# One-hots of the gate products: from keys outermost, eight tokens innermost, to token by token with the keys innermost

## The reference, cut to what matters

```python
q = (x @ w_q).reshape(T, PEER_HEADS, 2, PEER_DQ_HALF)
s = jnp.einsum('thpd,hpnd->thpn', q, sub_keys)
s1, i1 = lax.top_k(s[:, :, 0], PEER_TOPK)          # 16 of 128 keys, first half
s2, i2 = lax.top_k(s[:, :, 1], PEER_TOPK)          # 16 of 128 keys, second half
cand = s1[..., :, None] + s2[..., None, :]         # 256 sums per head
best, pos = lax.top_k(cand, PEER_TOPK)             # 16 experts per head, 8 heads
gate = jax.nn.softmax(best, axis=-1)
# per token 128 experts with index i1*128 + i2 and a gate
hb = gelu(einsum('tkd,td->tk', u[ids], xb))
out = einsum('tk,tkd->td', gate * hb, v[ids])
```

## Time and profile before

| | us |
|---|---|
| median of 3 runs | 4818.61 (4805.46 to 4823.8) |
| profiled execution | 4822.23 |
| its span, first to last instruction | 4820.7 |
| TensorE busy | 4335.7 (90%) |
| VectorE busy | 3214.2 (67%) |
| ScalarE busy | 1013.3 (21%) |
| gate stage of layer 0, about | 1438 to 1763 |
| gate stage of layer 1, about | 3666 to 3992 |

### The profile page before, as it was taken

How to read it: one execution, slowest core, us unless ns; L and a number is a source line. 1 busy time by engine, 2 the same in 40 slices (tenths; PEclk the granted TensorE clock), 3 DMA queues, 4 the chain that set the end, 5 groups by cost and what they waited for, 6 DMA issues and landing times. The chain is left out here.

```text
span 4820.7 us, 54964 instructions
## 1 busy us (share of the span) xinstructions
PE 4335.7 (90%) x19374; PEld 2495.3 (52%) x19374; DVE 3214.2 (67%) x6400; ACT 1013.3 (21%) x1581; POOL 712.3 (15%) x548
## 2 busy tenths in 40 slices
PE   8999998978979989999998877987778998989998
PEld 5777674645545545544444555554444554534443
DVE  1666652678978867766563675369997886866664
ACT  2111101122224431100001253213333441100000
POOL 0000000002221112222210000001221112322220
PEclk9999999989989999999999999999999999999999
DMA  4111141149877779999991100116776779999995
GB/s 146 38 40 39 39 134 56 54 164 356 322 296 263 282 285 387 374 377 391 394 363 65 33 1 31 44 52 234 284 281 234 281 276 352 400 392 390 392 402 196
DMA packets 291813, 1101.75 MB, mean 229 GB/s; under 512 B 30704, under 2 KB 131184, under 8 KB 222576
## 3 DMA queue, kind: packets, MB, share of 16 engines
q0 software_dynamic: 74752, 539.00, 28.4%
q1 hardware_dynamic: 148272, 336.40, 19.8%
q10 hardware_dynamic: 68544, 223.12, 12.0%
HBM read 1005.61 MB, written 92.80 MB: 228 GB/s over the span
## 5 line engine op out<-in xcount | busy, mean ns | idle before, releaser
L774 POOL DMA_INDIRECT room_p<-in_uv,ga_eidx_p x512 | 694.6, 1357 | 3308.1 <-DVEq L801 2106.5
L1311 PE MATMUL ex_psF_p<-ex_vst_p,ex_gh_p 128*128 128x512 f32 x1920 | 841.3, 593 | 18.4 <-DVE ex_gh_p L1405 18.4
L800 DVE SCALAR_TENSOR_TENSOR ga_acc_p<-room_p,ga_gw_p,ga_acc_p 128x1024 f32<-128x1024 f32 x504 | 625.2, 1282 | 21.5 <-issue 1.3
L786 DVE CUSTOM_DVE_ANT_0 room_p<-room_p,hx_p 128x1024 f32<-128x1024 f32 x512 | 605.6, 1220 | 8.9 <-DMA room_p<-in_uv,ga_eidx_p 4.9
L1311 PEld LDWEIGHTS ex_psF_p<-ex_vst_p,ex_gh_p 128*128 128x128 f32 x1920 | 363.3, 190 | 458.4 <-issue 454.0
L1311 PE MATMUL ex_psF_p<-ex_ust_p,ex_gh_p 128*128 128x512 f32 x1152 | 504.3, 596 | 14.3 <-DVE ex_gh_p L1405 14.3
L891 PE MATMUL eh_psH_sl_p<-h_hi_p,eh_uhi_sl_p 128*128 128x384 bf16 x1056 | 365.5, 346 | 164.9 <-DVE eh_ulo_sl_p L855 164.7
L1311 PEld LDWEIGHTS ex_psF_p<-ex_ust_p,ex_gh_p 128*128 128x128 f32 x1152 | 219.4, 191 | 294.4 <-issue 294.4
L891 PE MATMUL eh_psH_sl_p<-h_lo_p,eh_uhi_sl_p 128*128 128x384 bf16 x1056 | 364.1, 345 | 0.0
L891 PE MATMUL eh_psH_sl_p<-h_hi_p,eh_ulo_sl_p 128*128 128x384 bf16 x1056 | 363.4, 344 | 0.0
L1179 PE MATMUL gt_ps_p<-gt_ohh_p,gt_oh_p 128*128 128x128 bf16 x768 | 300.0, 391 | 51.5 <-DVEq L1164 51.5
(11 more groups left out here) (248 smaller groups left out, 6374.7 us busy)
## 6 DMA issues: line engine op xcount, KB each, us to landing
ex_vst_p<-in_uv ACTq DMA_DIRECT2D x160, 512.0 KB, 8.3
eh_ust_sl_p<-in_uT SPq DMA_DIRECT2D x132, 512.0 KB, 5.5
gates<-gt_gs_p ACTq DMA_DIRECT2D x24, 2048.0 KB, 7.9
ex_gst_p<-gates SPq DMA_DIRECT2D x128, 384.0 KB, 14.7
ex_ust_p<-in_uv ACTq DMA_DIRECT2D x96, 512.0 KB, 8.5
ex_est_p<-hidden SPq DMA_DIRECT2D x196, 192.0 KB, 14.7
eh_ust_gt_p<-in_uT SPq DMA_DIRECT2D x64, 512.0 KB, 6.6
ex_ust_p<-in_uT SPq DMA_DIRECT2D x60, 512.0 KB, 8.7
```

What stands on the lines that cost most here:

```text
L774: self.nc.gpsimd.indirect_dma_start(self.slot[s % self.RING], None, self.uv, bass.IndirectOffsetOnAxis(self.eidx[:, s:s + 1], 0)).then_inc ...
L786: nc.vector.tensor_tensor_reduce(out=row, in0=row, in1=self.hx[:, s // W, :], scale=1.0, scalar=0.0, op0=ALU.mult, op1=ALU.add, accum_out= ...
L800: nc.vector.scalar_tensor_tensor(acc[:], row, self.gw[:, s:s + 1], acc[:], op0=ALU.mult, op1=ALU.add)
L1311: last = nc.tensor.matmul(psF[:, t, x, :], gh[n % 3][:, P * t:P * t + P], vbuf[vslot[n]][:, BANK * x:BANK * x + BANK], start=(n == 0), sto ...
```

## The change

The keys are kept once, `[P, 128]`, in place of eight copies. The one-hots become `[partition, token, key]`, so the operand of token x, `[:, x, :]`, is 128 neighbouring bf16 elements. On VectorE the two sources of the compare change roles: before, the row of eight token values was repeated for every key (an outer repeat) against the replicated keys; now each token value is repeated 128 times innermost, and the row of keys is repeated for every token. In the two multiplications the gate part is repeated innermost in the same way. Counts of instructions, elements and matmuls, their order, and all waits stay as they are.

```diff
-        keys = sb("gt_keys", [P, NK, TI])
-        oh2 = [sb(f"gt_oh2{r}", [P, NK, TI]) for r in range(3)]
-        oh1 = sb("gt_oh1", [P, NK, TI])
+        keys = sb("gt_keys", [P, NK])
+        oh2 = [sb(f"gt_oh2{r}", [P, TI, NK]) for r in range(3)]
+        oh1 = sb("gt_oh1", [P, TI, NK])
...
-            nc.vector.tensor_copy(keys[:], cst.iota[:].unsqueeze(2).to_broadcast([P, NK, TI]))
+            nc.vector.tensor_copy(keys[:], cst.iota[:])
+            every = keys[:].unsqueeze(1).to_broadcast([P, TI, NK])
...
-                part = [pk[:, j, TI * n:TI * n + TI].unsqueeze(1).to_broadcast([P, NK, TI]) for j in range(4)]
-                nc.vector.tensor_tensor(oh1[:], part[0], keys[:], ALU.is_equal)
+                part = [pk[:, j, TI * n:TI * n + TI].unsqueeze(2).to_broadcast([P, TI, NK]) for j in range(4)]
+                nc.vector.tensor_tensor(oh1[:], part[0], every, ALU.is_equal)
...
-                nc.vector.tensor_tensor(oh2[n % 3][:], part[1], keys[:], ALU.is_equal)
+                nc.vector.tensor_tensor(oh2[n % 3][:], part[1], every, ALU.is_equal)
                 dve.drain()
                 nc.vector.tensor_tensor(ohh[n % 3][:], oh1[:], part[2], ALU.mult)
                 nc.vector.tensor_tensor(ohl[n % 3][:], oh1[:], part[3], ALU.mult)
...
-                    nc.tensor.matmul(o, oh2[n % 3][:, :, x], ohh[n % 3][:, :, x], start=True, stop=False)
+                    nc.tensor.matmul(o, oh2[n % 3][:, x, :], ohh[n % 3][:, x, :], start=True, stop=False)
...
-                    last = nc.tensor.matmul(o, oh2[n % 3][:, :, x], ohl[n % 3][:, :, x], start=False, stop=True)
+                    last = nc.tensor.matmul(o, oh2[n % 3][:, x, :], ohl[n % 3][:, x, :], start=False, stop=True)
```

More of the change, by code:

```diff
@@ L1130, in peer_gates @@
         sem = lambda n: nc.alloc_semaphore(n + tag)
-        keys = sb("gt_keys", [P, NK, TI])
-        oh2 = [sb(f"gt_oh2{r}", [P, NK, TI]) for r in range(3)]
-        oh1 = sb("gt_oh1", [P, NK, TI])
-        ohh = [sb(f"gt_ohh{r}", [P, NK, TI]) for r in range(3)]
-        ohl = [sb(f"gt_ohl{r}", [P, NK, TI]) for r in range(3)]
+        keys = sb("gt_keys", [P, NK])
+        oh2 = [sb(f"gt_oh2{r}", [P, TI, NK]) for r in range(3)]
+        oh1 = sb("gt_oh1", [P, TI, NK])
+        ohh = [sb(f"gt_ohh{r}", [P, TI, NK]) for r in range(3)]
+        ohl = [sb(f"gt_ohl{r}", [P, TI, NK]) for r in range(3)]
         gs = [sb(f"gt_gs{s}", [P, NK, TB], F32) for s in range(2)]
```

## The result

The changed kernel takes 4948.6 us (median, 4946.21 to 4952.81), against 4815.5 for the kernel before (median of four runs, the three of the table before and one more): a ratio of 1.0278, 95% interval 1.0256 to 1.030. Its profiled execution takes 4950.4 us, with a span of 4948.9. So the span grew by 128.2 us, where +115 had been worked out.

A forecast was written before the change was run, and what follows sets the result against it. TensorE was taken to bound the gate stages, VectorE some 60 us behind, then VectorE after the change. Stages of +56.4 and +56.1 us plus 3 us of remaining waits gave +115 on 4818.6: 4934 us, range 4904 to 4970.

The forecast's parts named there:

- The price of the one-hots: VectorE's four one-hot instructions: each goes from 688 to 1226 ns, adding 103.3 us per gate stage.
- the upper of two bounds: One-hot instruction on VectorE: 1226 ns if the pace of two elements is lost, against 688 ns if it survives.
- Who is late: Gate stages: VectorE becomes the limit at 7.75 us per unit, against 4.2 (at most 6.2) for TensorE.
- the 1 to 2 us put for what might stay: Gate stages: VectorE's waits for ScalarE that remain, 1 to 2 us per stage.
- TensorE's gain: Gate matmuls with contiguous operands: some 100 us less per stage, all but the last unit's share turned into waits.
- the lower bound: Gate matmul on TensorE costing in proportion to its columns: 0.054 us, a pair with the hidden matmul 0.217 us.
- The 4.2 us put for a unit: TensorE's time for a unit of 16 matmul pairs after the change, between 3.5 and 6.2 us.
- What follows it (copy, DMA of the gates, barrier) is unchanged: End of the gate stage, after the last copy from PSUM starts: no added time.
- The first: Rival, one-hots on VectorE: they keep 688 ns with the innermost repeat, 54 to 94 us saved, 4745 us; chance 0.08.
- The break-even of 245 ns: Added time per one-hot instruction on VectorE above which the kernel gets slower; 47 us per stage.
- The second: Rival, one-hots on VectorE: only two of the four lose the pace, about +5 us per stage, 4828 us; chance 0.03.
- The third: Rival, TensorE: layout not the cause, gate matmuls stay at 0.23 us; with fast one-hots 4819 us, chance 0.02.

The follow-up runs named there:

- taking the gain away: Changed kernel, but TensorE reads the one-hot tiles with the old step of eight elements: 4957.8 us, ratio 1.0289 to the kernel before.
- the kernel with pairs: Changed kernel, but each index and gate part is copied twice side by side and one-hot operations read the pairs: 4760.7 us, ratio 0.9888 to the kernel before.
- the kernel with two of four: Changed kernel, but the two compares read values laid down twice side by side, the multiplications repeat one value: 4853.5 us, ratio 1.0082 to the kernel before.

## Why the prediction was right, and where it was short

**The price of the one-hots** was taken at 1226 ns, the upper of two bounds, from the argument that a repeated value has no neighbour. Measured 1218 to 1225, and with neighbours given back 683 to 692. Right, and for the reason given.

**Who is late.** VectorE: the chain from the first one-hot to the end of the last takes 373.4 us in both stages, where 372.2 and 372.5 had been worked out. Its waits inside are gone, as forecast; the 1 to 2 us put for what might stay were not needed, but 0.12 us of idle time now stands before some 15 more of the low parts, where a wait had covered it: 1.8 us per stage.

**TensorE's gain.** At full clock 0.22 us per pair, the lower bound. The 4.2 us put for a unit came near the mean, 218.85 / 48 = 4.6 us of busy time, but by luck: the reason given, weights that must load beside a short stream, does not show, since a unit at full clock takes 16 x 0.22 = 3.5 us. What raises the mean is the clock, named in the prediction further down: at 1.2 GHz a unit takes 16 x 0.43 = 6.9 us. The last copy starts 5.09 and 4.84 us after the last one-hot's end, where 4.3 had been put. That the rest turns into waiting was shown by taking the gain away (+6 and +5 us).

**The step that failed** is the sentence "What follows it (copy, DMA of the gates, barrier) is unchanged": +6.1 and +6.5 us. The prediction had named the gathered pairs as queued behind the one-hots and had seen that the last unit of TensorE follows at once, but did not ask when the last pair's refill is then sent: with the last gates, on the same DMA engines. Held back, the gap is 9.8 us. In the profiled execution this is where the 128 us differ from the 115 (12.6 of 13.2); what the collision costs the whole kernel is less sure, since holding the refill back did not lower the time by as much.

**The rivals.** The first (VectorE keeps its pace) was priced at 4745 us; the kernel with pairs is that case, 4761 us, with three copies per stage and a like collision more. The break-even of 245 ns per instruction came out at about 225 in the kernel with two of four. The second (compares and multiplications differ) fell with the four equal lines. The third fell with the 0.22 us.

## What to carry to other kernels

A layout that suits TensorE is written by someone: price the writer's operations in the new order before the reader's gain, and ask which of the two the stage waits for. A 16-bit value that must be repeated innermost can be laid down as a pair first; the two-source operation then keeps two elements per step (683 to 692 ns here, in place of 1218 to 1225), for one small copy (688 ns per 128 tokens). When the limit moves to another engine, look at the end of the stage as well: what that engine frees last is sent last, beside what the stage's end waits for.

## What the runs showed of the hardware that was not expected

The price of a stepped moving operand does not follow TensorE's clock. At a step of eight the gate matmul holds the next one off for 0.21 us at full clock and 0.23 at half (kernel before, with the granted clock of 0.50), where contiguous columns cost 0.055 and 0.11 (changed kernel, 1811.43 to 1811.54). So the step costs nearly four times at 2.4 GHz and twice at 1.2 GHz:

```profile
1442.50:1443.50 1.00, 1.00 (x5) 0.53 (x5) 1.00 (x1) 0.00 (x0) 0.00 (x0) 0.50 0.06 25
```

```profile
1442.89 0.41 PE L1181 MATMUL gt_ps_p<-gt_ohl_p,gt_oh_p 128*128 128x128 bf16 x1
1443.12 0.50 PE L891 MATMUL eh_psH_gt_p<-h_lo_p,eh_uhi_gt_p 128*128 128x384 bf16 x1
```

At a step of four it is 0.10 us at full clock and 0.12 at half, where it hardly differs from contiguous columns:

```profile
1717.96 0.31 PE L1190 MATMUL gt_ps_p<-gt_ohh_p,gt_oh_p 128*128 128x128 bf16 x1
1718.08 0.51 PE L891 MATMUL eh_psH_gt_p<-h_hi_p,eh_uhi_gt_p 128*128 128x384 bf16 x1
```
